# Score products of a chunked RWKV-7 scan in 64x64 tiles, with the masked quarter left out

## The reference, cut to what matters

```python
def wkv7_scan(r, w, k, v, kk, a, s0):
    def step(S, inp):
        r_t, w_t, k_t, v_t, kk_t, a_t = inp
        s_kk = jnp.einsum('zbhvk,zbhk->zbhv', S, kk_t)
        S = (S * w_t[..., None, :] - s_kk[..., None] * (kk_t * a_t)[..., None, :]
             + v_t[..., :, None] * k_t[..., None, :])
        return S, jnp.einsum('zbhvk,zbhk->zbhv', S, r_t)
```

## Time and profile before

| | |
|---|---|
| median of three runs | 2407.59 us (2403.31 to 2408.84) |
| profiled execution | 2401.35 us, span 2399.4 us |
| mean granted TensorE clock | 0.983 |
| PE busy | 2243.7 us, 94% |
| PEld busy | 1282.6 us, 53% |
| DVE busy | 936.9 us, 39% |
| ACT busy | 397.0 us, 17% |
| POOL busy | 167.3 us, 7% |

### The profile page before, as it was taken

How to read it: one execution, slowest core, us unless ns; L and a number is a source line. 1 busy time by engine, 2 the same in 40 slices (tenths; PEclk the granted TensorE clock), 3 DMA queues, 4 the chain that set the end, 5 groups by cost and what they waited for, 6 DMA issues and landing times. The chain is left out here.

```text
span 2399.4 us, 56100 instructions
## 1 busy us (share of the span) xinstructions
PE 2243.7 (94%) x23412; PEld 1282.6 (53%) x23412; DVE 936.9 (39%) x1965; ACT 397.0 (17%) x685; POOL 167.3 (7%) x162
## 2 busy tenths in 40 slices
PE   5998989999888889999999999889998999999997
PEld 2446777777676765544444444545555444444444
DVE  2357666676757621211111111479613111111113
ACT  2022323232323201000000000211312000000001
POOL 1001010100101000000000000000000000000000
PEclk8998999999999999999999999899999999999999
DMA  9981010101000035799999999502036999999995
GB/s 369 386 316 32 2 33 2 32 2 32 13 22 21 2 122 197 268 383 393 395 396 393 394 396 390 193 1 70 1 140 255 395 397 394 393 397 393 392 392 172
DMA packets 181670, 538.56 MB, mean 224 GB/s; under 512 B 12545, under 2 KB 54145, under 8 KB 181410
## 3 DMA queue, kind: packets, MB, share of 16 engines
q1 hardware_dynamic: 175202, 515.16, 55.8%
q0 software_dynamic: 6336, 21.63, 3.8%
HBM read 510.81 MB, written 25.95 MB: 224 GB/s over the span
## 5 line engine op out<-in xcount | busy, mean ns | idle before, releaser
L2108 PE MATMUL ps<-raw,xs 128*64 128x512 f32 x3072 | 673.8, 596 | 4.0 <-PEq L2102 3.9
L2108 PEld LDWEIGHTS ps<-raw,xs 128*64 128x64 f32 x3072 | 217.7, 137 | 431.0 <-issue 429.6
L2120 PE MATMUL ps<-raw,xs 128*32 128x256 f32 x6144 | 342.3, 380 | 3.2 <-PEq L2102 3.2
L2120 PEld LDWEIGHTS ps<-raw,xs 128*32 128x32 f32 x6144 | 195.1, 110 | 134.0 <-issue 10.4
L2299 DVE SCALAR_TENSOR_TENSOR h<-h,ps 128x768 f32<-128x768 f32 x32 | 30.5, 954 | 461.9 <-DVEq L2298 461.9
L1644 DVE COPY_PREDICATED wk<-m,ps 128x128 f32<-128x128 uint8 x360 | 101.4, 352 | 116.4 <-DVEq L1640 116.2
L2426 PE MATMUL ps<-h,raw 128*128 128x512 f32 (+1 forms) x448 | 124.7, 440 | 7.2 <-PEq L2417 7.2
L2227 ACT ACTIVATE h<-ps 128x768 f32<-128x768 f32 x32 | 25.9, 811 | 595.1 <-ACTq L2226 595.1
L900 PE MATMUL ps<-h,wk 128*128 128x512 f32 (+1 forms) x416 | 121.4, 438 | 1.5 <-PEq L1216 1.3
L1030 PE MATMUL ps<-wk 64*64 64x64 f32 x2400 | 102.9, 223 | 14.5 <-PEq L1006 13.8
L1044 PE MATMUL ps<-wk 64*64 64x64 f32 x2400 | 98.5, 219 | 5.0 <-PEq L1006 3.2
(11 more groups left out here) (333 smaller groups left out, 2643.9 us busy)
## 6 DMA issues: line engine op xcount, KB each, us to landing
raw<-in_moe_w_gate SPq DMA_DIRECT2D x64, 2048.0 KB, 18.0
raw<-in_moe_w_up SPq DMA_DIRECT2D x64, 2048.0 KB, 20.0
raw<-in_moe_w_down SPq DMA_DIRECT2D x64, 2048.0 KB, 19.1
wk<-in_mod_w SPq DMA_DIRECT2D x24, 2048.0 KB, 12.1
wk<-in_ev_w_in SPq DMA_DIRECT2D x18, 512.0 KB, 5.3
raw<-in_od_w_in SPq DMA_DIRECT2D x4, 2048.0 KB, 15.2
hrow<-rows SPq DMA_DIRECT2D x10, 512.0 KB, 2.9
ysum<-low SPq DMA_DIRECT2D x10, 512.0 KB
```

The lines of the kernel that those rows point to most:

```text
L2108: last = pe.matmul(ps[to:to + CAPS, bank_of(kind, ee)], XS[ee][:, c, 0:CAPS], raw[:, slot(l, 2 * m + c // 4), c % 4, 8 * to:8 * to + 512], ...
L2120: last = pe.matmul(ps[to:to + 32, bank_of(kind, ee) + 1, 0:256], XS[ee][:, c, CAPS:], raw[:, slot(l, 2 * m + c // 4), c % 4, 8 * to:8 * to ...
```

## The change

The four products of a direction become eight. Each is in a 64x64 tile: the source tokens are split in two halves (`to:te`), the half that gives the weight columns and the output partitions. One half needs all 128 target tokens for both target features (256 columns, `a, b = 0, P`); in the forward direction that is the first half, in the backward direction the second. The other half needs only the 64 target tokens of its own half (2 x 64 columns); the rest of it, a quarter of each score matrix, lies wholly outside the triangle and is left out. PSUM keeps there what an earlier product left, and the mask multiplies it by zero. So that no odd bit pattern stands there at first, DVE sets partitions 0 to 63 of bank 5 to zero once, before the first `ymean_read`. Nothing else changes; DVE still multiplies full banks.

```diff
@@ -974,9 +974,11 @@
                                 if n >= 4:
                                     pe.wait_ge(sem("mat_read"), 2).then_inc(sem("mat_read"), -2)
                                 for k, src in enumerate((nb, kp)):
-                                    for hh in range(2):
-                                        lo, hi = hh * HD, hh * HD + HD
-                                        last = pe.matmul(ps[:, 4 + (n + 2 + hh) % 4, k * 256:(k + 1) * 256], src[lo:hi, z, tt], ar[lo:hi, z, tt], start=True, stop=True)
+                                    for to, te in HALF[::1 - 2 * z]:
+                                        a, b = (0, P) if to == z * HD else (to, te)
+                                        for hh, (lo, hi) in enumerate(HALF):
+                                            out = ps[to:te, 4 + (n + 2 + hh) % 4, k * 256:(k + 1) * 256].rearrange("p (u n) -> p u n", u=2)
+                                            last = pe.matmul(out[:, :, a:b], src[lo:hi, z, tt, to:te], ar[lo:hi, z, tt, :, a:b], start=True, stop=True)
                                 last.then_inc(sem("mat_ready"), 2)
                                 n += 2
                             if tt == 0:
@@ -1724,6 +1726,8 @@
                     shift(VV)
                     bonus_input()
                     take_mods(dve, EARLY, PARTS, 5)
+                    dve.memset(ps[0:HD, 5], 0.0).then_inc(dve_done, 1)
+                    done()
                     dve.sem_inc(sem("ymean_read"), 1)
                     for l, n in ((0, 1), (1, 0), (1, 1)):
                         take_gain(dve, l, n)
```

## The result

The changed kernel takes 2410.68 us (median of 12 runs, 2404.82 to 2415.09) against 2405.57 us for the kernel before in the same runs (12 runs, 2402.23 to 2416.9): a ratio of 1.0024, 95% interval 1.0012 to 1.0035. It is slower by about 5.8 us, between 2.9 and 8.4. The prediction had no change as likeliest and gave slower 0.09. The profiled execution of the changed kernel took 2404.82 us, the least of its twelve, with a span of 2403.0 us, 3.6 us more than the one of before.

What follows compares the result with a forecast made beforehand. It took the TensorE-DVE chain in the score phases, from a direction's first record to DVE's start, as the bound. Phases -0.8 us plus memset +0.7 made -0.1, carried to the 2407.59 us median: 2407.5 us, range 2402 to 2412.

Steps and rivals of the forecast that it cites:

- rival of tiles that take turns: Score products: tiles of one row half run in turn, +0.43 us a direction, +1.9 a phase, 2419.7 us; chance 0.07.
- rival of a faster set of products: Score products: direction's time falls by a quarter, 2404.5 us (chance 0.05), or halves, 2399.8 us (chance 0.06).
- 18.5 us each: Score phases: as a sign that the forecast is right, six phases of about 18.5 us each.
- the signal: `mat_ready` after a direction's last product: follows the slower tile, so DVE's start remains bound to the full product.
- early signal: `mat_ready` given at the part tile's end, about 0.35 us sooner: 2404.5 us, within 0.2%; chance 0.04.
- the size: One score phase: earlier DVE starts at tt=2, 3 and 4 sum to -0.13 us.
- -0.8 us over six phases: Score phases of all six pairs: -0.13 us each, in all -0.8 us; ends 0 and -1.5 us.
- the memset: DVE before the first `ymean_read`: 0.5 us plus 0.25 wait holds TensorE by 0.75; +0.7 us taken.
- the lower bound (+0.4): Memset's hold in the first phase: if the clock rises at the same moment as now, only +0.4 us is left.
- Rival 4: First phase: the clock after the memset's pause costs +3 us, 2410.5 us; chance 0.06.
- the products themselves: Score products, four become eight per direction: streaming stays 0.85 us, first step 0.27 instead of 0.32 us, 0.05 gained from rest.
- theory A: Follow-up theory, not in the prediction: the memset's pause shifts everything and the clock falls more often; +3 to +6 us for the memset alone.

Runs made afterwards that it cites:

- the padding: Kernel before with 64 more semaphore instructions on TensorE's queue in its pause ahead of the first phase's second direction, no product changed: 1.0011 (0.9998 to 1.0024), +2.6 us.

## Why the prediction was wrong

**Right: the score phase.** The tile that carries the length is unchanged. Timeline of the changed kernel in a narrow window:

```profile
324.32 0.67 PE L981 MATMUL ps<-wk 64*64 64x256 f32 x12
```

Twelve records in 0.67 us, full and part mixed. The direction has sixteen; their starts, read one by one and two at each time, are 324.32, 324.58, 324.80 and 325.02 for the full tiles, steps of 0.27, 0.22, 0.21 as forecast from the earlier trace rows, and 324.33, 324.49, 324.60, 324.71 for the part tiles beside them. The rival of tiles that take turns is refuted: 17.91 us a phase, not 19.9. So is the rival of a faster set of products. (The "18.5 us each" of the prediction ends at TensorE's next work, and holds for pairs two to six alone.)

**Right: the signal.** The signalling record starts at 324.72 and DVE at 325.59, 0.87 later, but 0.57 after the last full record. `mat_ready` waits for the slower tile, as read from the earlier trace rows; no early signal.

**Off: the size.** -0.08 us in an undisturbed phase instead of -0.13. The first step was 0.05 us shorter as forecast, but DVE started 0.57 after the last full record where it was 0.54 before (324.38 less 323.84). From the first record to DVE it is 1.27 us instead of 1.29, 0.02 gained and not 0.05. The remainder comes before the transposes, 0.05 us and not 0.025. And the -0.8 us over six phases was not there at all in the changed kernel: pairs two to six gave +0.1 (90.25 us against 90.14, and 90.22 against 90.14 in the second profiles). In the third pair DVE starts its masks with 0.80 us idle instead of 0.44, in the sixth it has 0.26 us without a releaser. Both come in all three profiles with one memset, before the 960th and the 1983rd record of VectorE, and in none without. With three memsets VectorE again waits longer at its 1983rd record, which is then another mask (0.59 us instead of 0.24). So VectorE has places of its own, and the memset's two instructions moved code onto them. Without the memset the gain of 0.08 was there.

**Right in sum, wrong in its parts: the memset.** It holds TensorE by 0.78 us, for 0.75, but since the clock rose at the same moment as before, the lower bound (+0.4) was the truth, 0.36 at DVE's tt=1. With the memset alone it was 0.50 at tt=1 and at the phase's end. The rest of the first phase's +0.75 in the changed kernel came with a stop, and wasn't there in the second profiles. Rival 4 is refuted: the lower clock of the first phase lasted 13.7 us in both kernels.

**Wrong: the sum had no term for the length of the program.** The step that failed is in "the products themselves", where four products become eight: I priced the 240 further products by array time alone, found it hidden, and took their 960 instructions to be free. They double the records of the score products, and they move all code behind them. Without the memset the tiles in all six pairs still cost +4.1 and +3.4 us. TensorE then stopped twice in the corrections of pairs two and five, 3.4 us in the first profile and 2.4 in the second; all its stops between 310 and 800 us were 3.8 and 3.2 us in the two profiles of before and 5.6 and 4.5 in those of the changed kernel. None of my rivals was this, and the "no gain, no loss" of tiles was read from TensorE's array, not from its instructions. That 2410.68 us lies inside the range of 2402 to 2412 is luck: the upper end stood for rival 4 and for the spread of the times, and neither brought it there.

**What adds up to the loss.** The stops alone don't. The table has the time between VectorE's last mask of the first pair and its last of the sixth, behind every hold and padding. Beside it stand the stops in that time (0.2 us and more, at the places described below) and the time that TensorE's granted clock was at the lower level.

| kernel | time, us | stops, us | lower clock, us |
|---|---|---|---|
| before, first and second profile | 573.8, 578.8 | 3.7, 5.1 | 6.8, 17.1 |
| one memset | 575.0 | 2.9 | 13.7 |
| three memsets | 575.3 | 4.2 | 6.8 |
| 64 more instructions | 573.6 | 2.2 | 13.7 |
| tiles from the third pair on | 575.9 | 3.0 | 17.1 |
| quarter left out from the third pair on | 572.3 | 1.6 | 10.2 |
| tiles, all columns | 579.2 | 6.1 | 17.1 |
| change without memset | 578.3 | 5.7 | 13.7 |
| the same, 96 more instructions | 576.9 | 4.2 | 10.2 |
| changed, first and second profile | 579.0, 582.5 | 6.3, 4.9 | 17.1, 27.3 |

As an estimate from these twelve profiles (a least-squares fit), the time is 567.7 us, plus 1.15 for each us of stops, plus 0.30 for each us at the lower clock, within 1.3 us. For the change that gives +1.4 us for stops (5.6 in the mean, for 4.4) and +3.1 for the clock (22.2 us, for 12.0), of +4.4 us in the means. The kernel with 96 more instructions has the tiles in all pairs but not the stops at the two places, and it is faster there than the other four profiles with tiles throughout.

The timed executions, which are many more, give the clock a smaller share. Its mean was 0.9796 in the 22 of the changed kernel for which the record has it beside 0.9809 in the 80 of the kernel before, and among executions of one kernel 0.001 less goes with 1.4 us more. That makes 1.8 us of the +5.8 (2.9 to 8.4) and +5.1 (2.6 to 7.7). With 0.4 to 0.75 for the memset's hold and 1.4 for stops the sum is +3.6 to +4.0: inside both intervals, with 1 to 2 us open.

Stops and clock aren't independent either. Of the 26 stops of 1.2 us or more between 210 and 910 us, in all thirteen profiles, six end 0.1 to 1.3 us before a stretch at the lower clock begins, two of them in the second profile of the changed kernel. So a part of what is booked to the clock may be a consequence of stops. No experiment separates them.

**Shown and not shown.** Shown: the stops hang on the place of the code and not on the products (the padding made the one of the second pair at the 6650th instruction; tiles from the third pair on have neither). The places lie on a grid of 256. Between 216 and 910 us the thirteen profiles have 55 idle times of 0.3 us and more, without a releaser and outside the score products, where most other profiles have none in the same code. They stand at 2753, 3009; 4858, 5114, 6650, 6906; 8757, 9013; 10547, 11059; 13932, 14188, 14956; 16549, 18085, 18597, 18853; 20190, 20958, 21726, 22750; 23708, 24220, 24476, or (6651, 18598, 22495) one record behind such a place. Within each group every difference is a whole multiple of 256, though TensorE's programs differ by up to 1520 instructions. From one group to the next the remainder shifts, which the trace doesn't explain.

Argued: that a stop is a wait for code. For it speak this grid, the two stops 256 apart in the fifth pair (18597, 18853) in each of the four profiles, the four more packets on the instruction queue, and that no wait of the kernel ends just before most of them. The Trainium skill ("Advanced Engine Details and Errata", ISA Cache) gives 16 KB for a line of 256 instructions, and with 1.38 MB in 84 packets, 16 KB each, the trace agrees. No view shows which packet TensorE waited for. Open as well: why most places of the grid bring no stop, the 1 to 2 us between sum and measurement, and how much of the clock's share follows from stops. The number of lower stretches in single profiles (2 and 5 for the kernel before, 5 for the memset alone, 6 for a kernel that lost nothing) doesn't sort the kernels by their time; their length is a part of it, as the table shows. And theory A isn't refuted for the memset's own share: its +1.9 us has an interval from -0.7 to +4.8.

## What to carry to other kernels

Before small tiles are used to leave work out, ask which tile carries the length: if each operand still sends its whole columns through one tile, the others only become idle. Count the instructions of a change that is written out, not just their time on the engine: the engine can stop for up to 2 us at fixed numbers of instructions, and every instruction added puts other code there. Count all stops on both sides, in every line, before a difference is put down to them. And one profile isn't the kernel: two executions of the same program differed by 4.6 us, more than the change seemed to be in its first profile.

## What the runs showed of the hardware

- Stops of TensorE without a releaser, up to 2.05 us long, at counts of instructions that lie whole multiples of 256 apart. A program has them at the same counts when it has them, but not each in every execution (2753 in one of two profiles of the kernel before). Most came in the corrections, where TensorE takes 32 records in 0.5 us, others in `keys` (1.0 and 1.3 us) and among the score products (0.26 us).
- VectorE has such places too: before its 1983rd record it stood 0.26 us without a releaser in each of three profiles with one memset, and at that number again with three.
- At the lower clock this stage lost about 0.30 us for each us (estimate from twelve profiles), and 0.001 of the mean granted clock went with 1.4 us of the whole time.
- With its score products halved, TensorE's clock fell to the lower level in the second and the fifth pair's phase, and those took 18.9 and 18.84 us instead of 16.8: with less work they were longer than the 17.99 us of before.
- A signal that stands on the last product in program order follows the slowest tile: the signalling part record started 0.30 us ahead of the last full one, and DVE 0.57 us after that.
- Semaphore instructions that the trace shows with 51 ns cost more in a row: on TensorE's queue one started 0.151 us after the other, 0.30 us for a pair of increment and wait, in both kernels with padding. 64 of them released the second direction at 9.64 us, 96 at 15.04.
